# Suffix sums of stick-breaking attention: one fp32 product against two products of a split operand

## The chip, the cores and the metric

The kernel runs on one core of a Trainium2 chip. The metric is device time of that core in microseconds (us), the median of three runs. The engines are named as the profile names them: PE (TensorE, with PEld for its weight loads), DVE (VectorE), ACT (ScalarE), POOL (GpSimd) and SP (SyncE).

## The reference, cut to what matters

The program is a transformer block (SwiGLU, two attentions, SwiGLU, an embedding gate) and four further mixers, at 512 tokens and width 1024. The change touches one of the two attentions of the first block, the stick-breaking one: 8 heads of 64.

```python
z = einsum('bhqd,bhkd->bhqk', q_blk, k) * scale
before = key_pos[None, :] < q_pos[:, None]
log_fail = where(before, log_sigmoid(-z), 0.0)
later = cumsum(log_fail, axis=3, reverse=True) - log_fail
log_a = log_sigmoid(z) + later
a = where(before, exp(where(before, log_a, 0.0)), 0.0)
out = einsum('bhqk,bhkd->bhqd', a, v)
```

With softplus(z) = max(z, 0) + ln(1 + exp(-|z|)), log_fail is -softplus(z), and log_a is z minus the sum of softplus over this key and all later ones. That sum is a product with a triangle of -1 (inside a block of 128 keys) and with a square of -1 (for the later blocks).

## The kernel before

All dense layers run as tiles of 8 k-blocks of weights 128x128. For each k-block `mm3` (L311 on) issues three products of 128x512 (L313 to L315) in the type fp32r, from a weight split in a rounded part `wh` and its rest `wl`. ACT makes `wh` (`split_hi`, L270), DVE makes `wl` (`split_lo`, L280), both three tiles ahead, and DVE takes the result of a tile out of PSUM.

The stage that matters is `mix_in`: 24 tiles that give q, k and v of 16 heads. Its tiles 4 to 14 have the stick-breaking attention woven in. A plan written out by hand, `plan`, says what runs beside which tile: "t" is a transposition of v (L1457, copied out by L1471), "s" a step of the stick-breaking attention, "c" a step of the other attention. `pe_amid` puts the PE part of a step behind a k-block of the tile: of two entries in a tile the first comes behind block 4 and the second behind block 8; of three, behind blocks 2, 5 and 8; a single one behind block 8. The steps in the plan stand so: s0 s1 in tile 4, s2 in 5, s3 s4 in 6, s5 in 7, s6 s7 in 8, s8 in 9, s9 s10 in 10, s11 s12 in 11, s13 in 12, s14 s15 in 13, s16 s17 in 14, s18 in 15; t1, t2, t3, t4 precede the s-steps of tiles 6, 9, 12, 15.

A unit u is a pair of heads and a block of 128 keys (kb = 3, 2, 1, 0), so units of 256, 512, 768 and 1024 columns follow one another, four times over. Its work goes through the engines in order:

- PE, step u: scores z into two PSUM banks (L1327), before that a wait for the weights of unit u-2
- ACT, step u: Abs, Exp, Ln (L1376, L1378, L1380)
- DVE, step u: max(z, 0) plus that (L1365), into the buffer `softplus` of the whole pair
- POOL, step u: a select that zeroes the masked part of the diagonal block (L1395)
- PE, step u+1, behind z of unit u+1: the suffix sums c (L1337), for each of two heads one fp32 product for each key block from kb to 3, added onto z in PSUM: 1, 2, 3 or 4 products for each head, 128 to 512 columns wide
- ACT, step u+1: Exp into `weights` (L1387); POOL selects again (L1401); PE, step u+2: times v (L1350)

The queues are in order. For tile k ACT issues: `split_hi` of tile k+3 (it waits until PE is through with tile k-1, whose buffer it fills), then the steps of tile k. DVE issues: `split_lo` of tile k+3 (it waits for that `split_hi`), then the steps of tile k, then the evacuation of tile k (L1512, L1520, L1523). At steps 6, 10, 14 and 18 DVE also copies a finished pair out of PSUM (L1358), first in the step. POOL runs only the selects and sums of squares here. After tile 23 come the last "c" steps, and then the product with `w_out`.

Of the kernel before, what the change touches and what calls it, by code (L numbers as in the profile page):

```python
# [25 lines left out]
F32 = mybir.dt.float32  # L26
F32R = mybir.dt.float32r
I32 = mybir.dt.int32
ALU = mybir.AluOpType
ACT = mybir.ActivationFunctionType  # L30

P = 128
SEQ = 512
D = 1024
DB = D // P
TB = SEQ // P
# [17 lines left out]
def kernel_program(nc, I, out):  # L54
    top = ExitStack()
    with top:
        def sem(name):
            return top.enter_context(nc.semaphore(name))

        def sb(name, shape, dt=F32, ctx=top):  # L60
            return ctx.enter_context(nc.sbuf_tensor(name, shape, dt))
# [111 lines left out]
        for name, n, src in stages:  # L173
            first[name] = len(tile_stage)
            for k in range(n):
# [4 lines left out]
                if name == "ple" and k % 2:  # L180
                    kb = PLE // P
                elif name.endswith("_down"):
                    kb = min(WB, FB - WB * (k % DOWN))
                else:
                    kb = DB
# [439 lines left out]
        for nm in ("g_ffn1_pre", "g_ffn1_post", "g_mix_pre", "g_mix_post", "g_ffn2_pre", "g_ffn2_post", "g_ple_post",  # L625
                   "g_out_sb", "g_out_ch", "norm_w_2", "final_norm_w_2", "conv_w_conv_2"):
            a = I[nm]
            if len(a.shape) == 1:
                v = a.rearrange("(r c) -> r c", c=P)
            elif len(a.shape) == 2:  # L630
                v = a.rearrange("a (r c) -> (a r) c", c=P)
# [649 lines left out]
        with ExitStack() as c:  # L1281
# [4 lines left out]
            bias = sb("bias", [P, H8, SEQ], ctx=c)  # L1286
            osq = sb("out_squares", [P, 4, SEQ], ctx=c)
            osum = sb("out_square_sums", [P, 2, SEQ], ctx=c)
            tri = sb("tri", [P, 2, P], ctx=c)
            tmp = sb("softplus_parts", [P, 4, SEQ], ctx=c)  # L1290
            ch_room = sb("ch_room", [P, 6, SEQ], ctx=c)
            off = {3: 0, 2: P, 1: 3 * P, 0: 6 * P}
            wide = 10 * P
            SP_ = sb("softplus", [P, 2, wide], ctx=c)
            A = sb("weights", [P, 2, wide], ctx=c)
            b_back = sem("bias_back")
            (n_sq, n_sum, n_mm, n_ms, n_inv, n_rt, n_sp, n_rs, n_f) = (sem(f"mixnorm_{x}") for x in (
                "sq", "sum", "mm", "ms", "inv", "root", "spread", "rstd", "f"))
            (sbc, z_mm, abs_d, exp_d, ln_d, sp_raw, sp_d, c_mm, a_raw, a_d, av_mm, o_d) = (sem(f"sb_{x}") for x in (
                "const", "z", "abs", "exp", "ln", "spraw", "sp", "c", "araw", "a", "av", "o"))  # L1300
            ntri, nones = tri[:, 0, :], tri[:, 1, :]
            ev_mix = n["ev"]
            sb_units = [(pair, kb) for pair in range(4) for kb in (3, 2, 1, 0)]
# [3 lines left out]
            def sb_z(u):  # L1307

                b0 = 4 if u % 2 == 0 else 2
                return banks8[:, b0:b0 + 2, 0:SEQ - sb_units[u][1] * P]  # L1310

            def v_cols(slot, x, s):

# [2 lines left out]
            def sb_pe(pe, s):  # L1316
                if s < SU:
                    pair, kb = sb_units[s]
                    slot, z = pair % 3, sb_z(s)
                    if kb == 3:  # L1320
                        pe.wait_ge(evac, ev_mix + 3 * pair + 2)
                    if s == 1:
                        pe.wait_ge(evac, ev_mix + HEAD + 1)
                    if s >= 2:
                        pe.wait_ge(a_raw, s - 1)
                    for r in range(2):
                        pe.matmul(z[:, r, :], qk[HD * r:HD * r + HD, slot, 1, kb * P:kb * P + P],  # L1327
                                  qk[HD * r:HD * r + HD, slot, 0, kb * P:SEQ], start=True, stop=True).then_inc(z_mm, 1)
                if 1 <= s < SU + 1:
                    u = s - 1  # L1330
                    kb, z = sb_units[u][1], sb_z(u)
                    if u == 0:
                        pe.wait_ge(sbc, 2)
                    pe.wait_ge(sp_d, u + 1)
                    for r in range(2):
                        for k2 in range(kb, TB):
                            m = pe.matmul(z[:, r, (k2 - kb) * P:SEQ - kb * P], ntri if k2 == kb else nones,  # L1337
                                          SP_[:, r, off[k2]:off[k2] + SEQ - k2 * P],
                                          start=False, stop=True, skip_group_check=True)
                    m.then_inc(c_mm, 1)  # L1340
                if 2 <= s < SU + 2:
                    u = s - 2
                    pair, kb = sb_units[u]
                    if kb == 3:
                        pe.wait_ge(taken, taken0 + pair + 1)
                        if pair:
                            pe.wait_ge(o_d, pair)
                    pe.wait_ge(a_d, u + 1)
                    for r in range(2):
                        pe.matmul(ps[OUT][HD * r:HD * r + HD, kb * P:SEQ], v_cols(pair % 3, kb, r),  # L1350
                                  A[:, r, off[kb]:off[kb] + SEQ - kb * P],
                                  start=kb == 3, stop=kb == 0, skip_group_check=True).then_inc(av_mm, 1)

            def sb_dve(dve, s):
                if s >= 6 and s % 4 == 2:
                    pair = s // 4 - 1
                    dve.wait_ge(av_mm, 8 * pair + 8)
                    nc.vector.tensor_copy(F[:, pair, :], ps[OUT][:, :]).then_inc(o_d, 1)  # L1358
                if s < SU:
                    kb = sb_units[s][1]  # L1360
                    w = SEQ - kb * P
                    dve.wait_ge(ln_d, s + 1)
                    if s >= 4:
                        dve.wait_ge(c_mm, s // 4 * 4)
                    nc.vector.scalar_tensor_tensor(out=SP_[:, :, off[kb]:off[kb] + w], in0=sb_z(s),  # L1365
                                                   scalar=0.0, in1=tmp[:, 2 * (s % 2):2 * (s % 2) + 2, 0:w], op0=ALU.max,
                                                   op1=ALU.add).then_inc(sp_raw, 1)

            def sb_act(act, s):
                if s < SU:  # L1370
                    w = SEQ - sb_units[s][1] * P
                    t = tmp[:, 2 * (s % 2):2 * (s % 2) + 2, 0:w]
                    act.wait_ge(z_mm, 2 * s + 2)
                    if s >= 2:
                        act.wait_ge(sp_raw, s - 1)
                    nc.scalar.activation(t, sb_z(s), ACT.Abs).then_inc(abs_d, 1)  # L1376
                    act.wait_ge(abs_d, s + 1)
                    nc.scalar.activation(t, t, ACT.Exp, scale=-1.0).then_inc(exp_d, 1)  # L1378
                    act.wait_ge(exp_d, s + 1)
                    nc.scalar.activation(t, t, ACT.Ln, bias=1.0).then_inc(ln_d, 1)  # L1380
                if 1 <= s < SU + 1:
                    u = s - 1
                    kb = sb_units[u][1]
                    act.wait_ge(c_mm, u + 1)
                    if u >= 4:
                        act.wait_ge(av_mm, u // 4 * 8)
                    nc.scalar.activation(A[:, :, off[kb]:off[kb] + SEQ - kb * P], sb_z(u), ACT.Exp).then_inc(a_raw, 1)  # L1387

            def sb_pool(pool, s):

                if s < SU:
                    kb = sb_units[s][1]
                    v = SP_[:, :, off[kb]:off[kb] + P]
                    pool.wait_ge(sp_raw, s + 1)
                    nc.gpsimd.affine_select(out=v, in_=v, compare_op=ALU.is_gt, fill=0.0, base=0,  # L1395
                                            pattern=[[0, 2], [1, P]], channel_multiplier=-1).then_inc(sp_d, 1)
                if 1 <= s < SU + 1:
                    kb = sb_units[s - 1][1]
                    v = A[:, :, off[kb]:off[kb] + P]
                    pool.wait_ge(a_raw, s)  # L1400
                    nc.gpsimd.affine_select(out=v, in_=v, compare_op=ALU.is_gt, fill=0.0, base=0,  # L1401
                                            pattern=[[0, 2], [1, P]], channel_multiplier=-1).then_inc(a_d, 1)
# [139 lines left out]
                                            ALU.add).then_inc(n_sum, 1)  # L1542

            def pool_tail(pool):
                nc.gpsimd.memset(nones, -1.0).then_inc(sbc, 1)
                pool.wait_ge(sbc, 1)
                nc.gpsimd.affine_select(out=ntri, in_=nones, compare_op=ALU.is_ge, fill=0.0,
                                        base=0, pattern=[[-1, P]], channel_multiplier=1).then_inc(sbc, 1)
                for s in range(SU + 3):
                    sb_pool(pool, s)  # L1550
                    if s >= 6 and s % 4 == 2:
                        pool.wait_ge(o_d, s // 4)
                        out_sums(pool, 0, s // 4 - 1)

                pool.wait_ge(b_back, 16 * (P // COPIES))
                nc.gpsimd.memset(bias[0:HD, :, SEQ - HD:SEQ], NEG).then_inc(sbc, 1)
                pool.wait_ge(n_sum, 3)
                for s in range(CU + 5):
                    ch_pool(pool, s)
                    if s >= 8 and s % 4 == 0:  # L1560
                        pool.wait_ge(o_taken, g_ch + s // 4 - 1)
                        out_sums(pool, 1, s // 4 - 2)
# [1313 lines left out]
```

## Time and profile before

| | us |
|---|---|
| median of 3 runs | 2346.49 |
| lowest, highest | 2342.91, 2348.24 |
| the profiled execution | 2341.71 |
| its span | 2339.9 |
| PE busy | 2211.8 (95%) |
| PE weight loads busy | 1776.7 (76%) |
| DVE busy | 1127.8 (48%) |
| ACT busy | 854.7 (37%) |
| POOL busy | 412.3 (18%) |

A row of the timeline gives the start of an instruction (or of a run of the same ones, with x their number), how long it took, and in brackets the idle time of its engine before it with what ended it. The time of a matmul in the profile is from its start to its modelled end; the pace of products is read from start to start. An fp32 product leaves two records, one in fp32r leaves one. PEclk is the granted clock of PE: 1.00 is 2.4 GHz, 0.50 is 1.2 GHz.

### The profile page before, as it was taken

The numbers are of one execution on the slowest core, as the hardware profiler recorded it, in microseconds if no ns is written. First come the engines' busy times: TensorE is split into PE (matmuls) and PEld (weight loads), VectorE is DVE, ScalarE is ACT, GpSimd is POOL, SyncE is SP. The second block draws the span as 40 slices with busy tenths as digits, with TensorE's granted clock in tenths as the row PEclk, the third lists the DMA queues.
The fourth block names the chain that finished last, engine by engine and source line by source line (L and its number), as shares of the span: only waits on it lengthen the run. The fifth ranks groups of instructions, "written<-read, shape, count | busy, mean of one in ns | idle before, by whom it ended". The sixth has DMA issues, their size and how long they took to land. (4 is left out here: it accounts for less than half of the span.)

```text
span 2339.9 us, 29203 instructions
## 1 busy us (share of the span) xinstructions
PE 2211.8 (95%) x10830; PEld 1776.7 (76%) x10830; DVE 1127.8 (48%) x1805; ACT 854.7 (37%) x1405; POOL 412.3 (18%) x459
## 2 busy tenths in 40 slices
PE   7999999999889999998899999999999997899989
PEld 6888887666677888887788878886777886776657
DVE  5444324423436444324575543346565775655433
ACT  4322223443334322223432241135445753433453
POOL 2111003112423111001210010002100241014441
PEclk8999999999989999999999999999999996999999
DMA  4333333411022333331333256740242220233202
GB/s 135 116 93 96 95 97 84 95 45 55 19 72 72 108 97 94 97 94 50 109 90 99 72 91 97 101 72 1 72 119 74 68 58 10 73 86 73 48 18 70
DMA packets 359321, 182.12 MB, mean 78 GB/s; under 512 B 41925, under 2 KB 356014, under 8 KB 358830
## 3 DMA queue, kind: packets, MB, share of 16 engines
q1 hardware_dynamic: 359214, 180.69, 31.0%
q8 instruction: 68, 1.11, 0.2%
q14 instruction: 39, 0.32, 0.0%
HBM read 176.14 MB, written 4.52 MB: 77 GB/s over the span
## 5 line engine op out<-in xcount | busy, mean ns | idle before, releaser
L313 PE MATMUL ps<-xh,wh 128*128 128x512 f32 x1920 | 766.0, 399 | 10.8 <-DVE wl L280 4.2
L315 PE MATMUL ps<-xh,wl 128*128 128x512 f32 x1920 | 749.3, 390 | 0.0
L314 PE MATMUL ps<-xl,wh 128*128 128x512 f32 x1920 | 748.5, 390 | 0.0
L280 DVE TENSOR_TENSOR wl<-raw,wh 128x1024 fp32r<-128x1024 f32 x334 | 422.6, 1266 | 435.7 <-ACT wh L270 431.0
L270 ACT ACTIVATE wh<-raw 128x1024 fp32r<-128x1024 f32 x334 | 342.1, 1027 | 375.3 <-PE ps L315 332.1
L313 PEld LDWEIGHTS ps<-xh,wh 128*128 128x128 f32 x1920 | 360.9, 188 | 102.9 <-issue 22.2
L315 PEld LDWEIGHTS ps<-xh,wl 128*128 128x128 f32 x1920 | 360.7, 188 | 77.3
L314 PEld LDWEIGHTS ps<-xl,wh 128*128 128x128 f32 x1920 | 361.1, 188 | 73.0 <-issue 2.4
L458 PE MATMUL ps<-xh,wh 128*128 128x512 f32 x304 | 129.9, 427 | 25.4 <-ACT xh L393 15.6
L451 POOL TENSOR_TENSOR acc<-acc,sq 128x512 f32<-128x512 f32 x72 | 102.6, 1424 | 273.1 <-ACT sq L836 178.0
L313 PE MATMUL ps<-a_hi,wh 128*128 128x512 f32 x352 | 136.9, 389 | 0.0
L314 PE MATMUL ps<-a_lo,wh 128*128 128x512 f32 x352 | 136.9, 389 | 0.0
L315 PE MATMUL ps<-a_hi,wl 128*128 128x512 f32 x352 | 136.9, 389 | 0.0
L749 POOL TENSOR_TENSOR F<-F,rstd 128x512 f32<-128x512 f32 x44 | 57.1, 1299 | 400.8 <-ACT F L764 400.8
L459 PE MATMUL ps<-xh,wl 128*128 128x512 f32 x304 | 126.9, 417 | 0.0
L462 PE MATMUL ps<-xl,wh 128*128 128x512 f32 x304 | 91.6, 410 | 4.7 <-DVE xl L426 3.0
L458 PEld LDWEIGHTS ps<-xh,wh 128*128 128x128 f32 x304 | 62.7, 206 | 40.9 <-issue 26.6
L767 ACT ACTIVATE a_hi<-ps 128x512 f32 (+1 forms) x44 | 26.4, 599 | 163.8 <-DVE ps L787 163.8
L764 ACT ACTIVATE F<-ps 128x512 f32<-128x512 f32 x44 | 26.4, 599 | 150.7 <-DVE ps L784 150.7
L448 POOL COPY acc<-sq 128x512 f32<-128x512 f32 x12 | 8.8, 736 | 395.9 <-ACT sq L887 323.4
L315 PEld LDWEIGHTS ps<-a_hi,wl 128*128 128x128 f32 x352 | 66.1, 188 | 13.8
L313 PEld LDWEIGHTS ps<-a_hi,wh 128*128 128x128 f32 x352 | 66.1, 188 | 13.7
(380 smaller groups left out, 2560.7 us busy)
## 6 DMA issues: line engine op xcount, KB each, us to landing
raw<-in_w_ffn_gate SPq DMA_DIRECT2D x44, 512.0 KB, 3.8
raw<-in_w_ffn_up SPq DMA_DIRECT2D x44, 512.0 KB, 3.8
raw<-in_w_ffn_down SPq DMA_DIRECT2D x32, 512.0 KB, 3.8
raw<-in_conv_w_in SPq DMA_DIRECT2D x32, 512.0 KB, 4.0
raw<-in_fox_w_in SPq DMA_DIRECT2D x32, 512.0 KB, 9.9
raw<-in_gdn_w_in SPq DMA_DIRECT2D x32, 512.0 KB, 4.1
raw<-in_w_in SPq DMA_DIRECT2D x24, 512.0 KB, 3.8
raw<-in_swa_w_in SPq DMA_DIRECT2D x32, 256.0 KB, 3.8
```

What stands on the lines that cost most here:

```text
L270: nc.scalar.activation(wh[s][:, 0:kb, :], raw[r][:, 0:kb, :], ACT.Copy).then_inc(hi_done, 1)
L280: nc.vector.tensor_tensor(wl[s][:, 0:kb, :], raw[r][:, 0:kb, :], wh[s][:, 0:kb, :].bitcast(F32), ALU.subtract).then_inc(lo_done, 1)
L313: pe.matmul(o, wh[s][:, kb, :], x_hi, start=start, stop=False)
L314: pe.matmul(o, wh[s][:, kb, :], x_lo, start=False, stop=False)
L315: return pe.matmul(o, wl[s][:, kb, :], x_hi, start=False, stop=stop)
L451: nc.gpsimd.tensor_tensor(acc[:, :], acc[:, :], sq[:, b % 2, :], ALU.add).then_inc(acc_done, 1)
L458: pe.matmul(ps[g][:, :], wh[s][:, b, :], x_hi[:, b, :], start=b == 0, stop=False)
L459: pe.matmul(ps[g][:, :], wl[s][:, b, :], x_hi[:, b, :], start=False, stop=False)
L462: last = pe.matmul(ps[g][:, :], wh[(t + g) % SPLIT][:, b, :], x_lo[:, b, :], start=False, stop=b == DB - 1)
L749: nc.gpsimd.tensor_tensor(SR[:, s, :], S[:, s, :], rstd[:, :], ALU.mult).then_inc(sr_done, 1)
L764: nc.scalar.activation(S[:, s, :], ps[ffn_bank(i, j)][:, :], ACT.Silu).then_inc(silu_done, 1)
L767: nc.scalar.activation(act_hi[:, bass.ds(p, 1), :], ps[ffn_bank(i, j)][:, :].rearrange("p (o q) -> p o q", o=1), ACT.Copy).then_inc(up_hi, 1)
```

## The change

The softplus of a unit is written into `softplus_parts` in place of a buffer of its own, and masked there. From it ACT makes a rounded copy `softplus_hi` in fp32r, at the end of its step u, behind the weights of unit u-1; DVE makes the rest, `softplus_lo`, as the first work (behind a pair's copy) of its step u+1. The triangle and the square of -1 are fp32r, in which they are exact. PE then issues two fp32r products in place of each fp32 one, first the rounded part and then the rest, with the widest key block last instead of first. PE waits for `softplus_lo` where it waited for the select. The `weights` buffer holds two units in turn in place of a pair. Abs and Exp now count on one semaphore, Ln and the rounded copy on another. Nothing changes in the plan.

```diff
@@ -1286,18 +1286,19 @@
             bias = sb("bias", [P, H8, SEQ], ctx=c)
             osq = sb("out_squares", [P, 4, SEQ], ctx=c)
             osum = sb("out_square_sums", [P, 2, SEQ], ctx=c)
-            tri = sb("tri", [P, 2, P], ctx=c)
+            tri = sb("tri", [P, 2, P], F32R, ctx=c)
             tmp = sb("softplus_parts", [P, 4, SEQ], ctx=c)
             ch_room = sb("ch_room", [P, 6, SEQ], ctx=c)
             off = {3: 0, 2: P, 1: 3 * P, 0: 6 * P}
             wide = 10 * P
-            SP_ = sb("softplus", [P, 2, wide], ctx=c)
-            A = sb("weights", [P, 2, wide], ctx=c)
+            sp_hi = sb("softplus_hi", [P, 2, wide], F32R, ctx=c)
+            sp_lo = sb("softplus_lo", [P, 2, wide], F32R, ctx=c)
+            A = sb("weights", [P, 4, SEQ], ctx=c)
             b_back = sem("bias_back")
             (n_sq, n_sum, n_mm, n_ms, n_inv, n_rt, n_sp, n_rs, n_f) = (sem(f"mixnorm_{x}") for x in (
                 "sq", "sum", "mm", "ms", "inv", "root", "spread", "rstd", "f"))
-            (sbc, z_mm, abs_d, exp_d, ln_d, sp_raw, sp_d, c_mm, a_raw, a_d, av_mm, o_d) = (sem(f"sb_{x}") for x in (
-                "const", "z", "abs", "exp", "ln", "spraw", "sp", "c", "araw", "a", "av", "o"))
+            (sbc, z_mm, abs_exp, ln_hi, sp_raw, sp_d, sp_parts, c_mm, a_raw, a_d, av_mm, o_d) = (sem(f"sb_{x}") for x in (
+                "const", "z", "absexp", "lnhi", "spraw", "sp", "parts", "c", "araw", "a", "av", "o"))
             ntri, nones = tri[:, 0, :], tri[:, 1, :]
             ev_mix = n["ev"]
             sb_units = [(pair, kb) for pair in range(4) for kb in (3, 2, 1, 0)]
@@ -1308,6 +1309,12 @@
 
                 b0 = 4 if u % 2 == 0 else 2
                 return banks8[:, b0:b0 + 2, 0:SEQ - sb_units[u][1] * P]
+
+            def sb_t(u, w):
+                return tmp[:, 2 * (u % 2):2 * (u % 2) + 2, 0:w]
+
+            def sb_a(u, w):
+                return A[:, 2 * (u % 2):2 * (u % 2) + 2, 0:w]
 
             def v_cols(slot, x, s):
 
@@ -1331,12 +1338,13 @@
                     kb, z = sb_units[u][1], sb_z(u)
                     if u == 0:
                         pe.wait_ge(sbc, 2)
-                    pe.wait_ge(sp_d, u + 1)
+                    pe.wait_ge(sp_parts, u + 1)
                     for r in range(2):
-                        for k2 in range(kb, TB):
-                            m = pe.matmul(z[:, r, (k2 - kb) * P:SEQ - kb * P], ntri if k2 == kb else nones,
-                                          SP_[:, r, off[k2]:off[k2] + SEQ - k2 * P],
-                                          start=False, stop=True, skip_group_check=True)
+                        for k2 in range(TB - 1, kb - 1, -1):
+                            for part in (sp_hi, sp_lo):
+                                m = pe.matmul(z[:, r, (k2 - kb) * P:SEQ - kb * P], ntri if k2 == kb else nones,
+                                              part[:, r, off[k2]:off[k2] + SEQ - k2 * P],
+                                              start=False, stop=True, skip_group_check=True)
                     m.then_inc(c_mm, 1)
                 if 2 <= s < SU + 2:
                     u = s - 2
@@ -1348,7 +1356,7 @@
                     pe.wait_ge(a_d, u + 1)
                     for r in range(2):
                         pe.matmul(ps[OUT][HD * r:HD * r + HD, kb * P:SEQ], v_cols(pair % 3, kb, r),
-                                  A[:, r, off[kb]:off[kb] + SEQ - kb * P],
+                                  sb_a(u, SEQ - kb * P)[:, r, :],
                                   start=kb == 3, stop=kb == 0, skip_group_check=True).then_inc(av_mm, 1)
 
             def sb_dve(dve, s):
@@ -1356,47 +1364,60 @@
                     pair = s // 4 - 1
                     dve.wait_ge(av_mm, 8 * pair + 8)
                     nc.vector.tensor_copy(F[:, pair, :], ps[OUT][:, :]).then_inc(o_d, 1)
+                if 1 <= s < SU + 1:
+                    u = s - 1
+                    kb = sb_units[u][1]
+                    w = SEQ - kb * P
+                    o = off[kb]
+                    dve.wait_ge(ln_hi, hi_of(u))
+                    nc.vector.tensor_tensor(sp_lo[:, :, o:o + w], sb_t(u, w), sp_hi[:, :, o:o + w].bitcast(F32),
+                                            ALU.subtract).then_inc(sp_parts, 1)
                 if s < SU:
-                    kb = sb_units[s][1]
-                    w = SEQ - kb * P
-                    dve.wait_ge(ln_d, s + 1)
-                    if s >= 4:
-                        dve.wait_ge(c_mm, s // 4 * 4)
-                    nc.vector.scalar_tensor_tensor(out=SP_[:, :, off[kb]:off[kb] + w], in0=sb_z(s),
-                                                   scalar=0.0, in1=tmp[:, 2 * (s % 2):2 * (s % 2) + 2, 0:w], op0=ALU.max,
+                    w = SEQ - sb_units[s][1] * P
+                    dve.wait_ge(ln_hi, ln_of(s))
+                    nc.vector.scalar_tensor_tensor(out=sb_t(s, w), in0=sb_z(s), scalar=0.0, in1=sb_t(s, w), op0=ALU.max,
                                                    op1=ALU.add).then_inc(sp_raw, 1)
+
+            def ln_of(u):
+                return 2 * u + 1
+
+            def hi_of(u):
+                return 2 * u + 2
 
             def sb_act(act, s):
                 if s < SU:
                     w = SEQ - sb_units[s][1] * P
-                    t = tmp[:, 2 * (s % 2):2 * (s % 2) + 2, 0:w]
+                    t = sb_t(s, w)
                     act.wait_ge(z_mm, 2 * s + 2)
                     if s >= 2:
-                        act.wait_ge(sp_raw, s - 1)
-                    nc.scalar.activation(t, sb_z(s), ACT.Abs).then_inc(abs_d, 1)
-                    act.wait_ge(abs_d, s + 1)
-                    nc.scalar.activation(t, t, ACT.Exp, scale=-1.0).then_inc(exp_d, 1)
-                    act.wait_ge(exp_d, s + 1)
-                    nc.scalar.activation(t, t, ACT.Ln, bias=1.0).then_inc(ln_d, 1)
+                        act.wait_ge(sp_parts, s - 1)
+                    nc.scalar.activation(t, sb_z(s), ACT.Abs).then_inc(abs_exp, 1)
+                    act.wait_ge(abs_exp, 2 * s + 1)
+                    nc.scalar.activation(t, t, ACT.Exp, scale=-1.0).then_inc(abs_exp, 1)
+                    act.wait_ge(abs_exp, 2 * s + 2)
+                    nc.scalar.activation(t, t, ACT.Ln, bias=1.0).then_inc(ln_hi, 1)
                 if 1 <= s < SU + 1:
                     u = s - 1
-                    kb = sb_units[u][1]
                     act.wait_ge(c_mm, u + 1)
-                    if u >= 4:
-                        act.wait_ge(av_mm, u // 4 * 8)
-                    nc.scalar.activation(A[:, :, off[kb]:off[kb] + SEQ - kb * P], sb_z(u), ACT.Exp).then_inc(a_raw, 1)
-
-            def sb_pool(pool, s):
-
+                    if u >= 2:
+                        act.wait_ge(av_mm, 2 * u - 2)
+                    nc.scalar.activation(sb_a(u, SEQ - sb_units[u][1] * P), sb_z(u), ACT.Exp).then_inc(a_raw, 1)
                 if s < SU:
                     kb = sb_units[s][1]
-                    v = SP_[:, :, off[kb]:off[kb] + P]
+                    act.wait_ge(sp_d, s + 1)
+                    if s >= 4:
+                        act.wait_ge(c_mm, s // 4 * 4)
+                    nc.scalar.activation(sp_hi[:, :, off[kb]:off[kb] + w], t, ACT.Copy).then_inc(ln_hi, 1)
+
+            def sb_pool(pool, s):
+
+                if s < SU:
+                    v = sb_t(s, P)
                     pool.wait_ge(sp_raw, s + 1)
                     nc.gpsimd.affine_select(out=v, in_=v, compare_op=ALU.is_gt, fill=0.0, base=0,
                                             pattern=[[0, 2], [1, P]], channel_multiplier=-1).then_inc(sp_d, 1)
                 if 1 <= s < SU + 1:
-                    kb = sb_units[s - 1][1]
-                    v = A[:, :, off[kb]:off[kb] + P]
+                    v = sb_a(s - 1, P)
                     pool.wait_ge(a_raw, s)
                     nc.gpsimd.affine_select(out=v, in_=v, compare_op=ALU.is_gt, fill=0.0, base=0,
                                             pattern=[[0, 2], [1, P]], channel_multiplier=-1).then_inc(a_d, 1)
@@ -1542,9 +1563,9 @@
                                             ALU.add).then_inc(n_sum, 1)
 
             def pool_tail(pool):
-                nc.gpsimd.memset(nones, -1.0).then_inc(sbc, 1)
+                nc.gpsimd.memset(nones.bitcast(F32), -1.0).then_inc(sbc, 1)
                 pool.wait_ge(sbc, 1)
-                nc.gpsimd.affine_select(out=ntri, in_=nones, compare_op=ALU.is_ge, fill=0.0,
+                nc.gpsimd.affine_select(out=ntri, in_=nones.bitcast(F32), compare_op=ALU.is_ge, fill=0.0,
                                         base=0, pattern=[[-1, P]], channel_multiplier=1).then_inc(sbc, 1)
                 for s in range(SU + 3):
                     sb_pool(pool, s)
```

## Rows read from the trace of the kernel before

**Rows 1.** Windows: stretch, length, PE, PEld, DVE, ACT, POOL busy, PEclk, DMA, GB/s.

```profile
427.00:548.00 121.00, 120.19 (x542) 80.21 (x542) 35.83 (x42) 54.27 (x74) 19.04 (x37) 1.00 0.26 61
```

**Rows 2.** By tile: one line of kernel each, durations minimum/median/maximum in ns, forms.

```profile
L1337 PE MATMUL ps<-softplus,tri x160: 272/379/697, 430.3 to 545.2; 128*128 128x128 f32 x64, 128*128 128x256 f32 x48, 128*128 128x384 f32 x32, 128*128 128x512 f32 x16
L1365 DVE SCALAR_TENSOR_TENSOR softplus<-ps,softplus_parts x16: 423/824/1225, 428.9 to 538.1; 128x256 f32<-128x256 f32 x4, 128x512 f32<-128x512 f32 x4, 128x768 f32<-128x768 f32 x4, 128x1024 f32<-128x1024 f32 x4
...
L1378 ACT ACTIVATE softplus_parts<-softplus_parts x16: 416/738/1057, 428.0 to 535.9; 128x256 f32<-128x256 f32 x4, 128x512 f32<-128x512 f32 x4, 128x768 f32<-128x768 f32 x4, 128x1024 f32<-128x1024 f32 x4
```

**Rows 3.** Timeline of unit 15, from its scores to its suffix sums.

```profile
533.69 1.13 PE L1327 MATMUL ps<-qk_slots 64*128 64x512 f32 x4
...
534.75 2.87 PE L1337 MATMUL ps<-softplus,tri 128*128 128x384 f32 x12
...
537.54 0.65 PE L1350 MATMUL ps<-weights,v_tokens 128*64 128x256 f32 x4
...
538.13 1.23 DVE L1365 SCALAR_TENSOR_TENSOR softplus<-ps,softplus_parts 128x1024 f32<-128x1024 f32 x1 [5.58 <-ACT softplus_parts L1380]
538.69 1.05 ACT L270 ACTIVATE wh<-raw 128x1024 fp32r<-128x1024 f32 x1
...
539.43 0.41 POOL L1395 TENSOR_SCALAR_AFFINE_SELECT softplus<-softplus 128x256 f32<-128x256 f32 x1 [3.69 <-DVE softplus L1365]
...
539.87 1.41 DVE L280 TENSOR_TENSOR wl<-raw,wh 128x1024 fp32r<-128x1024 f32 x1
...
540.98 4.47 PE L1337 MATMUL ps<-softplus,tri 128*128 128x512 f32 x16
...
545.39 0.87 PE L1350 MATMUL ps<-weights,v_tokens 128*64 128x384 f32 x4
```

**Rows 4.** Timeline: the pace of fp32r products, and of weight loads without columns behind.

```profile
425.31 0.40 PE L315 MATMUL ps<-xh,wl 128*128 128x512 f32 x1
...
425.55 0.39 PE L313 MATMUL ps<-xh,wh 128*128 128x512 f32 x1
...
387.92 0.97 PEld L335 LDWEIGHTS ps<-ones,sq 128*128 128x128 f32 x8
```

**Rows 5.** Timeline: scores and suffix sums of units 2, 3, 7, 10 and 13 on PE.

```profile
436.46 0.92 PE L1327 MATMUL ps<-qk_slots 64*128 64x384 f32 x4
...
444.30 1.13 PE L1327 MATMUL ps<-qk_slots 64*128 64x512 f32 x4
...
445.36 2.87 PE L1337 MATMUL ps<-softplus,tri 128*128 128x384 f32 x12
...
451.43 4.58 PE L1337 MATMUL ps<-softplus,tri 128*128 128x512 f32 x16
...
473.32 1.13 PE L1327 MATMUL ps<-qk_slots 64*128 64x512 f32 x4
...
484.33 4.58 PE L1337 MATMUL ps<-softplus,tri 128*128 128x512 f32 x16
...
497.82 0.92 PE L1327 MATMUL ps<-qk_slots 64*128 64x384 f32 x4
...
504.56 2.87 PE L1337 MATMUL ps<-softplus,tri 128*128 128x384 f32 x12
...
522.78 0.70 PE L1327 MATMUL ps<-qk_slots 64*128 64x256 f32 x4
...
528.85 1.57 PE L1337 MATMUL ps<-softplus,tri 128*128 128x256 f32 x8
```

**Rows 6.** Timeline and windows: two waits of PE of one length, and the clock beside them.

```profile
393.79 0.77 PE L458 MATMUL ps<-xh,wh 128*128 128x512 f32 x1 [2.71 <-ACT xh L393]
...
392.00:395.00 3.00, 1.21 (x3) 1.05 (x4) 2.93 (x5) 1.30 (x3) 1.37 (x2) 0.54 0.87 235
...
1792.57 1.05 PE L2259 MATMUL ps<-ones,gdn_slots 128*128 128x1 f32 x8 [2.71 <-ACT gdn_slots L2089]
...
1792.00:1796.00 4.00, 3.43 (x19) 3.01 (x20) 3.93 (x9) 3.31 (x5) 0.00 (x0) 1.00 0.52 135
```

More of the change, by code:

```diff
@@ L1371, in sb_act @@
                     w = SEQ - sb_units[s][1] * P
-                    t = tmp[:, 2 * (s % 2):2 * (s % 2) + 2, 0:w]
+                    t = sb_t(s, w)
                     act.wait_ge(z_mm, 2 * s + 2)
                     if s >= 2:
-                        act.wait_ge(sp_raw, s - 1)
-                    nc.scalar.activation(t, sb_z(s), ACT.Abs).then_inc(abs_d, 1)
-                    act.wait_ge(abs_d, s + 1)
-                    nc.scalar.activation(t, t, ACT.Exp, scale=-1.0).then_inc(exp_d, 1)
-                    act.wait_ge(exp_d, s + 1)
-                    nc.scalar.activation(t, t, ACT.Ln, bias=1.0).then_inc(ln_d, 1)
+                        act.wait_ge(sp_parts, s - 1)
[4 more added lines that the diff above has]
+                    nc.scalar.activation(t, t, ACT.Ln, bias=1.0).then_inc(ln_hi, 1)
                 if 1 <= s < SU + 1:
                     u = s - 1
-                    kb = sb_units[u][1]
                     act.wait_ge(c_mm, u + 1)
-                    if u >= 4:
-                        act.wait_ge(av_mm, u // 4 * 8)
-                    nc.scalar.activation(A[:, :, off[kb]:off[kb] + SEQ - kb * P], sb_z(u), ACT.Exp).then_inc(a_raw, 1)
+                    if u >= 2:
+                        act.wait_ge(av_mm, 2 * u - 2)
+                    nc.scalar.activation(sb_a(u, SEQ - sb_units[u][1] * P), sb_z(u), ACT.Exp).then_inc(a_raw, 1)
+                if s < SU:
+                    kb = sb_units[s][1]
+                    act.wait_ge(sp_d, s + 1)
+                    if s >= 4:
+                        act.wait_ge(c_mm, s // 4 * 4)
+                    nc.scalar.activation(sp_hi[:, :, off[kb]:off[kb] + w], t, ACT.Copy).then_inc(ln_hi, 1)
             def sb_pool(pool, s):
                 if s < SU:
-                    kb = sb_units[s][1]
-                    v = SP_[:, :, off[kb]:off[kb] + P]
+                    v = sb_t(s, P)
                     pool.wait_ge(sp_raw, s + 1)
```

## The prediction, made before the changed kernel was seen

> **What bounds the kernel now.** First the page: PE is busy 95% of the span, every other engine under half, so time is gained or lost on PE. Then the windows of the stage: from 427 to 548 us, where all sixteen units run, PE is busy 120.19 of 121 us at full clock, ACT 54 and DVE 36 [rows 1]. PE waits for nothing here. Each unit goes through a long chain PE, ACT, DVE, POOL, PE, but the plan puts enough tile products between its two ends. So two numbers decide: how much PE time the suffix sums give back, and whether the cover still holds a chain that grows by two operations and loses part of the cover. The tile and timeline views give both.
>
> **What PE gets back.** L1337 has 160 records, two for each fp32 product: 32 products of 128 columns, 24 of 256, 16 of 384, 8 of 512, 20,480 columns in all [rows 2]. Unit 15 has 2560 columns and takes 4.41 us up to the next product (540.98 to 545.39), unit 14 1536 columns and 2.79 us (534.75 to 537.54) [rows 3]. Four clocks for a column at 2.4 GHz make 4.27 and 2.56; the rest is mostly a change-over that stays. In all that is some 34.3 us.
> After the change there are 160 fp32r products. One of 512 takes 0.227 us to or from its neighbour (425.31 to about 425.55, with rounding), 0.213 of it columns [rows 4]. For 256 and 384 I take the columns and the same 0.013: 0.120 and 0.173. For 128 no fp32r row exists. Each product brings a weight load, and loads with only one column behind them go every 0.11 us, (0.97 - 0.19) / 7 [rows 4]; so a 128-wide product can't be expected under 0.112. Bounds: 0.053 (columns alone) and 0.215 (an fp32 product's four clocks). I take 0.112, the row nearest in what it does. Sum: 64 x 0.112 + 48 x 0.120 + 32 x 0.173 + 16 x 0.227 = 22.1 us. PE work falls by 12.2 us: by nothing in a unit of 256 columns (both heads), 0.36 us at 512, 0.97 at 768, 1.8 at 1024.
> The weight-load row shows 0.11 us. The Trainium skill, TensorE: Matmul & The Clock Gate, section LDWEIGHTS, gives such a load its columns divided by 1.2 GHz, 107 ns, and the trace agrees; the same page's section Back-to-back issue gap gives a product its columns at 2.4 GHz plus 2.5 ns, 56 ns for 128. By that second rule alone the new sums would be an estimated 17.5 us and PE would get back 16.8.
>
> **What the chain becomes.** Unit 15, the plainest [rows 3]: scores start at 533.69; L1365 starts 4.44 us later and takes 1.23; the select ends at 539.84, 6.15 us after the scores. PE came for the sums at 540.98, 7.29 us after the scores, so there was 1.1 us to spare. New behind the select:
> - ACT's rounded copy. Nearest row: `split_hi`, 1.05 us for 1024 columns from and to the same kinds of memory [rows 3]; narrower ones as L1378, 0.42 to 1.06 [rows 2]. I take 1.03, 0.81, 0.60, 0.39 with 0.05 for each hand-over. ACT stands still for it from Ln to the end of the select.
> - DVE's subtraction. Nearest row: `split_lo`, two operands of 1024 columns, 1.41 us beside POOL's work in [rows 3]; I take 1.25, about L1365's 1.225 at that width [rows 2], and 0.97, 0.70, 0.43 for the others.
> Within a tile the widest chain is thus 6.15 + 0.05 + 1.03 + 0.05 + 1.25 + 0.05 = 8.58 us; in the same way 6.97 for 768, 5.36 for 512, 3.76 for 256.
> But the subtraction belongs to DVE's next step. Where that step is in the next tile, the subtraction stands behind `split_lo` of a later tile, which waits for `split_hi`, which now stands behind the rounded copy: 1.05 + 0.05 + 1.27 = 2.37 us more. Behind a pair's copy (L1358) or the copy of v (L1471) it is 0.68 more.
>
> **The sixteen units against their cover.** Cover is the distance from scores to sums on PE, less what the sums of the unit before give back.
> - Unit 15 (1024, next tile): 8.58 + 2.37 = 10.95 against 7.29 - 0.97 = 6.32. PE waits 4.6.
> - Unit 10 (768, next tile): 9.34 against 504.56 - 497.82 - 0.36 = 6.38 [rows 5]. Wait 3.0.
> - Units 13 and 5 (512, next tile, behind a pair's copy): 5.36 + 2.37 + 0.68 = 8.41 against 528.85 - 522.78 = 6.07 [rows 5]. Wait 2.35 each, 4.7 together; the rows of unit 5 stand at the same distance.
> - Unit 7 (1024, next tile, behind v's copy): 11.63 against 484.33 - 473.32 - 0.97 = 10.04 [rows 5]. Wait 1.6.
> - Unit 2 (768, next tile, behind v's copy): 6.97 + 2.37 + 0.68 = 10.02 against 445.36 - 436.46 - 0.36 = 8.54 [rows 5]. Wait 1.5, part of it at the transposition.
> - Unit 3 (1024, same tile): 8.58 against 451.43 - 444.30 - 0.97 = 6.16, and unit 2's wait of 0.9 lies in that cover [rows 5]. Wait 1.5.
> - Unit 0 (256, same tile): 3.76 against three blocks (9 x 0.227) and two scores, about 3.2. Wait 0.5.
> - The other eight have more cover than chain: next tile at 256 or 512 columns with a whole tile or two between, or behind a wait just counted (6, 11, 14).
> Sum of waits 17.4 us, all new, against 12.2 given back: the stage ends 5.2 us later. Nothing queued behind on DVE or ACT makes PE wait further: the splits are three tiles ahead, and a tile's evacuation is wanted two tiles later. POOL's selects move with their inputs. The new copies and subtractions, 11.3 and 13.4 us of work, would be free as engine time; it's their place in the queues that costs. The v product's wait for its buffer is met early, and L1365 loses its wait for the sums of the pair before, which no one is late by. From tile 15 on nothing differs, so the shift goes through to the end.
>
> **The clock.** A wait of 2.71 us before 393.79 had PE at 1.2 GHz behind it (granted 0.54 in 392 to 395), one of 2.71 before 1792.57 did not (1.00 in 1792 to 1796) [rows 6]. Unit 15's 4.6 us is longer than both. I price one fall: 3 us at half clock, as the first of these rows shows, cost PE some 1.5 us of work, and as the row ends before the fall does I take 1.7 (an estimate); nothing is the lower bound, 6 us the upper, for falls at units 10 and 15 of twice that length each. The Trainium skill, same page, section HAM oscillation, says that waits between bursts bring the clock down and every burst starts slow; taken at its word at each wait over 2 us it would be the upper bound.
>
> **Sum.** 5.2 + 1.7 = 6.9 us. The profiled execution took 2341.7 us, so 2348.6 in its terms; it stands 4.8 us under the median of the runs, 2346.5, from which I forecast: 2353.4 us.
>
> **Rivals.**
> - The narrow products don't run at full rate (the change doesn't do all that it says). If 128 columns cost 0.215, the 64 of them take 6.6 us more, of which 2.9 falls into waits: 3.7 later, 2357. For it: no row shows a narrow fp32r product. Against it: nothing in the rows but the name of the type. Chance 0.2.
> - Break-even. The narrow products at 0.06 (3.3 us less, 1.4 of it eaten by longer waits), hand-overs and subtractions a tenth shorter (0.7) and no fall of the clock: 5.2 - 1.9 - 0.7 = 2.6 later, 2349. Chance 0.22.
> - Faster: the saving lands and the waits do not come. One mechanism: the subtraction isn't held up by `split_lo`, because DVE and ACT reach the next tile's splits before PE is through with the tile. That takes away up to 2.37 us at units 15, 10, 13, 5, 7, 2, so 4.6 + 3.0 + 4.7 + 1.6 + 1.5 shrinks to 2.3 + 0.6, with 2.0 for units 3 and 0: 4.9 against 12.2, 7.3 faster, 2339. It decides from waits under 12.2 us in all. Against it: `split_hi` waits for the end of the tile before, and the rows show it at 538.69, behind unit 15's other work [rows 3]. Chance 0.07.
> - The forecast, waits about 17 with little or one fall of the clock: 0.51, its own range 2350 to 2359.
>
> **Range and chances.** The bounds (narrow products at either end, subtraction at 1.41 us for + 0.9, clock 0 to 6) reach from 2348 to over 2362. The range of 2346.5 to 2361.5 leaves out most of the faster case and the worst of the clock. Some 0.2% (4.7 us) is about what a measurement of this kernel can tell from no change. The faster case gives 0.06 over that, break-even 0.22 within it with a sliver of the others, slower 0.72.
>
> **What would show it.** In the profile after: sums of 512 columns 0.227 us apart and of 128 about 0.112 (0.215 makes it the first rival); PE idle before the sums of units 15, 10, 13, 5, in this order, ended by the subtraction; DVE with `split_lo` directly ahead of the subtraction there; ACT idle about 1 us before each rounded copy; PE idle in the stage 15 to 20 us where it was 1. The forecast is wrong if that idle time is under 12 us, if the subtraction runs before `split_lo`, or if the shift at the end of tile 14 isn't the shift at the end of the kernel.

## The result

The changed kernel took 2358.8 us in the median of ten runs (2349.6 to 2362.0) against 2342.8 us for the kernel before in its ten (2339.7 to 2348.9); the ratio is 1.0049, interval 1.0033 to 1.0064, which is 11.5 us slower. The two medians stand further apart, 16.0 us: the times of the change fall into two groups (2349.6 to 2350.8 and 2356.0 to 2362.0), and the median lies in the upper one. Measured again beside the experiments the ratio was 1.0040 (1.0024 to 1.0056). The profiled execution of the change is one of the lower group (2350.3 us); its span is 2348.6 us, 8.7 over that of before.

In the windows (columns as in [rows 1]) the stage that had PE busy 120.19 of 121 us now leaves it idle for 14 us:

```profile
427.00:548.00 121.00, 106.67 (x509) 73.63 (x508) 46.68 (x57) 64.56 (x89) 18.30 (x36) 0.96 0.27 57
```

The waits of PE between 425 and 562 us (total, times, longest) name one releaser, DVE's subtraction:

```profile
PE ps L1345 <- DVE softplus_lo L1373: 15.4, 8, 4.2
PE ps L1478 <- DVE v_features L1533: 1.2, 1, 1.2
```

As the measure of the stage I take the start of unit 0's scores and the start of unit 15's product with v. Before, from the timeline:

```profile
427.01 0.49 PE L1327 MATMUL ps<-qk_slots 64*128 64x128 f32 x4
...
549.12 1.08 PE L1350 MATMUL ps<-weights,v_tokens 128*64 128x512 f32 x4
```

After:

```profile
426.37 0.49 PE L1334 MATMUL ps<-qk_slots 64*128 64x128 f32 x4
...
558.28 1.08 PE L1358 MATMUL ps<-weights,v_tokens 128*64 128x512 f32 x4
```

122.1 us have become 131.9: the stage is 9.8 us longer, and nearly all of it (8.7) is there at the end. Unit 15, which answers to [rows 3], shows the chain in full, from the timeline of the changed kernel:

```profile
539.54 1.13 PE L1334 MATMUL ps<-qk_slots 64*128 64x512 f32 x4
...
543.99 1.22 DVE L1378 SCALAR_TENSOR_TENSOR softplus_parts<-ps,softplus_parts 128x1024 f32<-128x1024 f32 x1 [5.71 <-ACT softplus_parts L1398]
...
545.29 0.41 POOL L1417 TENSOR_SCALAR_AFFINE_SELECT softplus_parts<-softplus_parts 128x256 f32<-128x256 f32 x1 [5.86 <-DVE softplus_parts L1378]
...
545.73 1.06 ACT L1410 ACTIVATE softplus_hi<-softplus_parts 128x1024 fp32r<-128x1024 f32 x1 [1.07 <-POOL softplus_parts L1417]
546.69 1.04 ACT L270 ACTIVATE wh<-raw 128x1024 fp32r<-128x1024 f32 x1
547.83 1.23 DVE L280 TENSOR_TENSOR wl<-raw,wh 128x1024 fp32r<-128x1024 f32 x1 [2.02 <-ACT wh L270]
548.97 1.22 DVE L1373 TENSOR_TENSOR softplus_lo<-softplus_parts,softplus_hi 128x1024 fp32r<-128x1024 f32 x1
...
550.25 0.33 PE L1345 MATMUL ps<-softplus_hi,tri 128*128 128x128 f32 x1 [4.22 <-DVE softplus_lo L1373]
```

The select ends 6.16 us after the scores, as before; then come the rounded copy, `split_hi`, `split_lo` and only then the subtraction, and PE has its sums 10.71 us after the scores.

The other long waits, with the scores of the same unit ahead of each, answer to [rows 5] (units 2, 3, 7, 10, 13; of unit 5, at 470.03, only the first product of its sums is shown):

```profile
436.32 0.92 PE L1334 MATMUL ps<-qk_slots 64*128 64x384 f32 x4
...
446.02 0.33 PE L1345 MATMUL ps<-softplus_hi,tri 128*128 128x128 f32 x1 [0.70 <-DVE softplus_lo L1373]
...
444.18 1.13 PE L1334 MATMUL ps<-qk_slots 64*128 64x512 f32 x4
...
452.73 0.33 PE L1345 MATMUL ps<-softplus_hi,tri 128*128 128x128 f32 x1 [1.55 <-DVE softplus_lo L1373]
...
470.03 0.33 PE L1345 MATMUL ps<-softplus_hi,tri 128*128 128x128 f32 x1 [1.98 <-DVE softplus_lo L1373]
...
474.44 1.13 PE L1334 MATMUL ps<-qk_slots 64*128 64x512 f32 x4
...
485.75 0.33 PE L1345 MATMUL ps<-softplus_hi,tri 128*128 128x128 f32 x1 [1.16 <-DVE softplus_lo L1373]
...
497.44 0.92 PE L1334 MATMUL ps<-qk_slots 64*128 64x384 f32 x4
...
507.17 0.47 PE L1345 MATMUL ps<-softplus_hi,tri 128*128 128x128 f32 x1 [3.32 <-DVE softplus_lo L1373]
...
525.52 0.70 PE L1334 MATMUL ps<-qk_slots 64*128 64x256 f32 x4
...
533.61 0.33 PE L1345 MATMUL ps<-softplus_hi,tri 128*128 128x128 f32 x1 [1.98 <-DVE softplus_lo L1373]
```

The products of unit 14 show the new pace, from 540.60 on one after the other (128, 128, 256, 256, 384, 384 columns for the first head, and from 541.52 on the same for the second):

```profile
540.60 0.33 PE L1345 MATMUL ps<-softplus_hi,tri 128*128 128x128 f32 x1
...
540.88 0.33 PE L1345 MATMUL ps<-softplus_hi,tri 128*128 128x256 f32 x1
...
541.17 0.34 PE L1345 MATMUL ps<-softplus_hi,tri 128*128 128x384 f32 x1
...
541.52 0.22 PE L1345 MATMUL ps<-softplus_hi,tri 128*128 128x128 f32 x1
...
541.69 0.33 PE L1345 MATMUL ps<-softplus_hi,tri 128*128 128x256 f32 x1
...
542.42 0.65 PE L1358 MATMUL ps<-weights,v_tokens 128*64 128x256 f32 x4
```

The unit takes 1.82 us to the next product, where the same unit took 2.79. And three windows show the clock behind three of the waits (PEclk is the third number from the end, behind the five engines):

```profile
505.00:514.00 9.00, 6.83 (x23) 5.19 (x24) 4.57 (x4) 4.06 (x5) 0.98 (x3) 0.62 0.20 58
...
534.00:538.00 4.00, 4.00 (x17) 3.07 (x17) 2.21 (x2) 1.59 (x3) 2.28 (x4) 0.57 0.38 109
...
551.00:555.00 4.00, 4.00 (x16) 2.89 (x14) 0.00 (x0) 0.35 (x1) 0.00 (x0) 0.57 0.28 85
```

They lie behind the waits of units 10, 13 and 15. Behind the waits of units 3 (1.55 us) and 5 (1.98 us), the next longest, no window of the trace shows a fall.

### The profile page after: what moved, and what is told of

It is laid out like the page before. It is cut to its first block and busy times, and to the rows that moved or that the text cites. A ratio compares the mean times of both kernels' runs of the same rounds, so it can differ in the third digit from the quotient of the medians.

```text
span 2348.6 us, 29237 instructions
## 1 busy us (share of the span) xinstructions
PE 2205.9 (94%) x10830; PEld 1776.3 (76%) x10830; DVE 1141.1 (49%) x1821; ACT 865.8 (37%) x1421; POOL 411.5 (18%) x459
## 5 line engine op out<-in xcount | busy, mean ns | idle before, releaser
L458 PE MATMUL ps<-xh,wh 128*128 128x512 f32 x304 | 130.2, 428 | 25.8 <-ACT xh L393 15.8
L451 POOL TENSOR_TENSOR acc<-acc,sq 128x512 f32<-128x512 f32 x72 | 102.5, 1423 | 273.3 <-ACT sq L836 178.0
L458 PEld LDWEIGHTS ps<-xh,wh 128*128 128x128 f32 x304 | 62.9, 207 | 41.1 <-issue 26.7
```

What stands on the lines that cost most here:

```text
L451: nc.gpsimd.tensor_tensor(acc[:, :], acc[:, :], sq[:, b % 2, :], ALU.add).then_inc(acc_done, 1)
L458: pe.matmul(ps[g][:, :], wh[s][:, b, :], x_hi[:, b, :], start=b == 0, stop=False)
```

## The experiments

**1. The products without the longer chain.** DVE writes the rounded softplus itself; the rest is a buffer of zeros.

```diff
-                    pe.wait_ge(sp_parts, u + 1)
+                    pe.wait_ge(sp_d, u + 1)
...
-                    nc.vector.scalar_tensor_tensor(out=sb_t(s, w), in0=sb_z(s), ...
+                    nc.vector.scalar_tensor_tensor(out=sp_hi[:, :, o:o + w], in0=sb_z(s), ...
```

> The 160 fp32r products of the change on the chain of before: DVE writes the rounded softplus itself, POOL masks it, PE waits for the select, and the second product of each pair reads a buffer of zeros, so the rest of the softplus is left out of the sums. Theory (products give back, the longer chain takes more): PE waits stay near those of before (about 1.5 us), the stage ends 10 to 12 us earlier, span about 2329. Rival (the fp32r products themselves or the change of type on PE cost more than was priced): gain under 6 us with no new waits.

Measured: ratio 0.9948 (0.9931 to 0.9966), 12 us faster. In the waits no sum of a unit waits for anything. The stage:

```profile
426.38 0.49 PE L1334 MATMUL ps<-qk_slots 64*128 64x128 f32 x4
...
536.32 1.08 PE L1359 MATMUL ps<-weights,v_tokens 128*64 128x512 f32 x4
```

109.9 us, 12.2 shorter than before. The products alone give back just what was priced. This run keeps the other parts of the change, the `weights` buffer of two units and the shared semaphores, so these cost nothing that shows here.

**2. The chain without the products.** The chain as in the change, and one fp32 product of the rounded part.

```diff
-                            for part in (sp_hi, sp_lo):
-                                m = pe.matmul(z[...], ntri if k2 == kb else nones, part[...],
+                            m = pe.matmul(z[...], (ntri if k2 == kb else nones).bitcast(F32), sp_hi[...].bitcast(F32),
```

> The chain of the change (rounded copy on ACT, subtraction on DVE, PE waits for the rest) with one fp32 product of the rounded part as before, so the rest is left out of the sums. Theory: PE waits about 15 us before the suffix sums of units 15, 10, 13, 5, less at 15 than in the change because unit 14's product covers 1 us more; the stage ends about 14 us later, span 2354 to 2359 with falls of the clock. Rival (the cost of the change lies in its products or clock alone): under 5 us later.

Measured: ratio 1.0102 (1.0079 to 1.0124), 24 us slower. Waits of PE and the stage:

```profile
PE ps L1344 <- DVE softplus_lo L1372: 12.0, 8, 3.2
```

and the timeline:

```profile
426.92 0.49 PE L1334 MATMUL ps<-qk_slots 64*128 64x128 f32 x4
...
564.99 1.08 PE L1357 MATMUL ps<-weights,v_tokens 128*64 128x512 f32 x4
```

138.1 us, 16.0 longer, near the 14 expected. But this isn't all waiting: the waits are 12.0 us where 15 were expected, and behind two of them, at units 5 and 15, the clock falls (PEclk 0.83 in the window 470 to 480, and this one):

```profile
556.00:562.00 6.00, 6.00 (x17) 2.73 (x15) 0.00 (x0) 0.65 (x1) 0.00 (x0) 0.74 0.17 51
```

In the change the same chain makes 15.4 us of waits. The 3.4 us more are cover that the quicker products no longer give: PE waits 1.16 us in the change against 0.19 here at unit 7, 4.22 against 3.23 at unit 15, 1.55 against 0.57 at unit 3 and 3.32 against 2.93 at unit 10, close to the 0.97 and 0.36 us by which the prediction shortened the cover. So runs 1 and 2 (-12.2 and +16.0 us in the stage) can't be added up: their sum of 3.8 us has falls of the clock in it and lacks these 3.4 us, and that it comes near the 4.1 us of run 3 is chance.

The profiled span is 26.7 us longer, so another 10.7 arose outside the stage. It goes with the clock: PEclk is 0.57 in 650 to 690 against 0.74 for about the same work before (634 to 674), 0.86 in 1120 to 1140 against 1.00 (1096 to 1116), and 0.91 in 1810 to 1830 against 1.00 (1785 to 1805). Why the clock fell there in this execution stays open.

**3. PE kept busy in the waits.**

```diff
+                    if u in FILL:
+                        pe.wait_ge(taken, taken0 + FILL[u][0])
+                        for _ in range(FILL[u][1]):
+                            pe.matmul(ps[TURN][:, :], ntri, xh[:, 0, :], start=True, stop=True)
                     pe.wait_ge(sp_parts, u + 1)
```

> The changed kernel with products whose result nobody reads, put into the waits of PE before the suffix sums of units 5, 7, 10, 13 and 15 (9, 5, 12, 9 and 17 of 512 columns, 0.227 us each, a little less than each wait), so that PE does not stand idle there. Theory (waits of 17 us less 12 given back, and falls of the clock on top): no stretch at 1.2 GHz between 420 and 560 us, stage 3 to 5 us shorter than in the change, 5 to 6 us over before, and the spread of the times of the change (2349.6 to 2362.0) narrows to its lower end. Rival (the clock plays no part): time as the changed kernel, ratio to before 1.005.

Measured: ratio 1.0015 (1.0001 to 1.0030), 3.5 us slower than before in place of 9 to 12. The interval is clear of that of the first measurement of the change (1.0033 to 1.0064) and overlaps a little with that of the second (1.0024 to 1.0056). Its windows where the changed kernel had lost the clock, and its stage:

```profile
500.00:514.00 14.00, 13.60 (x67) 9.67 (x66) 6.78 (x6) 8.87 (x12) 3.89 (x6) 1.00 0.13 37
530.00:538.00 8.00, 8.00 (x46) 5.69 (x46) 2.59 (x3) 4.36 (x6) 3.63 (x4) 1.00 0.22 67
546.00:555.00 9.00, 9.00 (x46) 6.05 (x45) 1.92 (x2) 2.08 (x2) 0.41 (x1) 1.00 0.17 49
```

The timeline:

```profile
425.94 0.49 PE L1335 MATMUL ps<-qk_slots 64*128 64x128 f32 x4
...
552.11 1.08 PE L1363 MATMUL ps<-weights,v_tokens 128*64 128x512 f32 x4
```

126.2 us: 4.1 over before, 5.7 under the change. The time up to the subtraction is no shorter, only what fills it differs: 52 products of 0.227 us make 11.8, and 3.5 us of waits are left, 15.3 in all against 15.4. No window between 420 and 560 us shows a lower clock. So the falls of the clock cost the change some 5.7 us in this stage, by one profile of each. One expectation failed: the times still spread from 2344.3 to 2359.1, so the waits of this stage are not what makes most of that spread.

**4. The subtraction ahead of the next `split_lo`.**

```diff
-                if 1 <= s < SU + 1:
+                if 1 <= s < SU + 1 and s - 1 not in LAST.values():
+                    sb_rest(dve, s - 1)
...
+                mix_evac_(dve, i, j, ev0)
+                if 4 * i + j in LAST:
+                    sb_rest(dve, LAST[4 * i + j])
```

> The changed kernel with one move: where a unit's next step lies in the next tile, DVE subtracts right behind the evacuation of the tile, ahead of the next split_lo instead of behind it. Theory (the subtraction's place behind split_hi and split_lo costs 2.4 us at units 15, 10, 13, 5, 7, 2): waits before the suffix sums fall to about 10 us, most left at units 3, 15 and 11, the stage ends 2 us earlier than in before, ratio 0.998 to 1.000. Rival (the two added operations alone make the wait): waits as in the change, within 2 us of its time.

Measured: ratio 0.9979 (0.9967 to 0.9991). The waits of PE:

```profile
PE ps L1345 <- DVE softplus_lo L1380: 7.0, 7, 2.3
```

A window of the same run:

```profile
445.00:460.00 15.00, 12.67 (x55) 8.84 (x54) 3.90 (x6) 8.23 (x11) 1.58 (x4) 0.77 0.12 35
```

And its timeline:

```profile
426.34 0.49 PE L1334 MATMUL ps<-qk_slots 64*128 64x128 f32 x4
...
547.68 1.08 PE L1358 MATMUL ps<-weights,v_tokens 128*64 128x512 f32 x4
```

The waits for the subtraction halve, from 15.4 to 7.0 (about 10 were expected), with not an operation less. The stage, 121.3 us, is 0.8 us shorter than before and not 2, as the clock falls behind the longest wait left, 2.33 us at unit 3. The rival, that the two added operations alone make all of the wait, is out; the 7.0 us left are theirs and the shorter cover's.

**5. And the scores two k-blocks ahead.** PE issues the scores 1.4 us before it comes for the sums of the unit before.

```diff
+                for kind, s in spot(k, b + AHEAD):
+                    if kind == "s":
+                        sb_pe(pe, s, 1)
```

> The run with the early subtraction, and PE besides issues each unit's scores two k-blocks (1.4 us) before it comes for the suffix sums of the unit before, so that the cover grows by 1.4 us. Theory (cover against chain): waits before the suffix sums 3 us in all, at most 1.1 at one unit, no fall of the clock between 420 and 560 us, stage 9 us earlier than in before, ratio 0.995 to 0.997, the full gain of the products nearly kept. Rival (what the early subtraction left is not cover but something else): under 2 us better than the run with the early subtraction alone.

> The changed kernel with only the scores two k-blocks ahead, the subtraction left behind split_lo. Theory (cover against chain): waits fall from 17 to about 8 us (3.2 at unit 15, 1.5 at unit 10, 1.0 at 5 and 13), stage 4 us earlier than in before, less what the clock takes at unit 15: ratio 0.998 to 1.000. Rival (the order on DVE alone matters): time as the changed kernel.

> The kernel of before with the scores two k-blocks ahead, as a control. Theory (before has no waits that more cover could remove but 1.2 us at one transposition): within 1.5 us of before. Rival (the earlier scores help for a reason of their own): 3 us or more faster.

Measured, in this order: 0.9960 (0.9944 to 0.9975) with both moves; 0.9987 (0.9974 to 0.9999) with the scores ahead alone; 0.9997 (0.9982 to 1.0013) for the kernel of before with them. The waits of PE of the first two (the third has none):

```profile
PE ps L1348 <- DVE softplus_lo L1383: 1.7, 3, 0.7
```

```profile
PE ps L1348 <- DVE softplus_lo L1376: 5.9, 5, 2.8
```

So 15.4 us of waits become 7.0 by one move, 5.9 by the other and 1.7 by both, and the control shows that the earlier scores are worth nothing where no chain is late. The stage, taken in the same way, is 112.6 us with both moves, 9.5 shorter than before where 9 were expected, and 120.6 with the scores ahead alone, 1.5 shorter, with falls of the clock behind its two longest waits (1.76 and 2.84 us, at units 10 and 15). With both the version beats both kernels, by 0.40% (9.4 us) against before.

**6. The change again**, on the chip of the last three.

> The changed kernel itself, beside the others on one chip, for its spread and its granted clock. Theory: ratio 1.003 to 1.006, PE waits 15 to 18 us, one to three stretches at 1.2 GHz between 500 and 560 us that the kernel before has not.

Measured: 1.0040 (1.0024 to 1.0056), PE waits of 15.4 us for the subtraction in its profile as well, and three falls of the clock in the stage. But they are not the three of the first profile: here they lie behind units 5 (ahead of the stretch expected; PEclk 0.57 in 470 to 478), 10 and 15 (0.68 in 512 to 516, 0.59 in 549 to 557), and behind unit 13 there is none (1.00 in 533 to 547), although PE waits 1.98 us at unit 5 and at unit 13 in both profiles.

Over all the profiles the stage has ten waits of 1.76 to 2.93 us; six have a fall behind them and four have none. All five waits above 3.2 us have one, and none of the shorter waits, up to 1.57 us, has. In the four profiles of the stage with no wait above 1.6 us (before, runs 1 and 3, both moves) and in the control the clock never falls.

Over its eleven runs the time goes with the granted clock of the run: 0.963 to 0.965 at 2349.8 to 2351.6 us, 0.960 or 0.961 at 2356.1 to 2357.9, 0.957 or 0.958 at 2361.5 and 2362.4. The kernel before goes the same way (0.968 at 2340.1, 0.962 at 2353.2), so part of the spread is not the change's.

## Why the prediction was right, and where not

Forecast were 2353.4 us in a range of 2346.5 to 2361.5, 6.9 us over before; measured are 2358.8, 11.5 us over by the ratio and 8.7 in the profiled executions. The mechanism came as forecast: PE work is given back, and the subtraction, late behind `split_lo`, makes new waits of PE that are longer in sum. The cost of the clock came out larger.

**PE work given back.** Forecast 12.2 us. The four kinds of unit now take 0.59, 1.12, 1.82 and 2.75 us up to the product with v; against 9.45 for the four before that is 6.28, or 12.7 us for the four pairs of heads, and run 1 measured 12.2. By kind of unit, from narrow to wide, 0.05, 0.39, 0.98 and 1.76 us are given back; forecast were nothing, 0.36, 0.97 and 1.8. The price of a narrow product, the widest unknown, came out near the value taken: the two products of 128 columns take 0.28 us for the first head (540.60 to 540.88) and 0.17 for the second (541.52 to 541.69), 0.225 on average, against 2 x 0.112 forecast and 2 x 0.215 for the first rival, which is out. A single one can take less than 0.112 us, which the prediction had ruled out: the product behind 541.52 starts at 541.58. A pair of 256 takes 0.29, where 2 x 0.120 was forecast. The prediction's other estimate, 17.5 us for all the new sums, used a figure that the Trainium skill, TensorE: Matmul & The Clock Gate, section Back-to-back issue gap, gives for an isolated product and says is too small for narrow ones in a stream with weight loads; the rows give about 21.6 us (34.3 - 12.7), near the 22.1 of the sum.

**The chain.** Forecast 10.95 us for unit 15, measured 10.71; for unit 10 9.34, measured 9.73; 13: 8.41 and 8.09; 7: 11.63 and 11.31; 2: 10.02 and 9.70; 3: 8.58 and 8.55. The waits of these six units were forecast, in the same order, at 4.6, 3.0, 2.35, 1.6, 1.5 (with the transposition) and 1.5; the rows give 4.2, 3.3, 2.0, 1.2, 0.7 and 1.55. Unit 5 repeats unit 13 (1.98), and unit 0 waits 0.45 where 0.5 was forecast; these are all eight waits of the trace. The sum of the new waits was 17.4 and is 15.8 (15.4 + 1.2, less the 0.8 us that PE waited at a transposition before). Waits less gain: forecast 5.2, by the rows 15.8 - 12.7 = 3.1, by the filled run 4.1.

**The clock.** This is the term that was mis-sized: 1.7 us, one fall, was taken from bounds of 0 and 6. The profile of the change has falls behind three of its waits, and filling them takes 5.7 us off the stage; the time moves by some 6 to 8 us (1.0015 against 1.0040 and 1.0049). I had counted a fall at unit 15 only, because a wait of 2.71 us had gone either way [rows 6]; unit 13's, of 2.0 us, was enough here. Four waits were forecast over 2 us, and in either profile of the change three of them have a fall behind; which of units 5 and 13 it is, is chance as far as the runs show. So one fall was too few, and the 5.7 us measured lie just under the upper bound of 6. The two errors, 1 to 2 us too much for the waits and 4 too little for the clock, have opposite signs; the first hides part of the second.

**The shift at the end.** As forecast nothing behind tile 14 takes it back: the stage is 9.8 us longer but starts 0.64 earlier, so its end comes 9.2 us later, and the end of the kernel 8.7. That it came out so exactly has luck in it: in run 1 12.8 us earlier at the end of the stage became 10.6 at the end of the kernel, and in run 2 15.9 us later became 26.7, with the clock falling elsewhere.

**The faster rival** named the right place: it said that without `split_lo` ahead of the subtraction the waits would stay under the gain. Run 4 made that so: 7.0 us of waits, under the gain of 12, and the time fell below that of before; in the change itself `split_lo` was ahead in every unit that crosses a tile.

## What to carry to other kernels

Ahead of trading one engine's work for two more operations in a chain that crosses engines, subtract for each unit the chain from the cover that its consumer has, with the queue position of each new operation: here 12 us of PE work were gained, and 16 us of waits came from a chain two operations longer, about half of them (15.4 to 7.0 us) from the place of a subtraction of at most 1.2 us, behind work for three tiles later. Count also that quicker work of the consumer covers less (3.4 us here). The move in the queue and 1.4 us more cover turned the loss into a gain of 9.4 of the 12 us. And on PE a wait can cost more than its length, as the clock may fall behind it: some 5.7 us here beside 16 of waits.

## What had not been expected of the hardware

DVE's two-operand work stretches beside POOL's. The rest of unit 14 (768 columns) took 1.53 us with POOL's L1557 (536.42 to 537.46) and then its L1562 running beside it, that of unit 10 0.94 us without; `split_lo` took 1.86 beside L1562, where the other 13 of its rows between 420 and 562 us, with no work of POOL beside them, took 1.21 to 1.23. From the timeline of the changed kernel:

```profile
395.57 1.35 POOL L451 TENSOR_TENSOR acc<-acc,sq 128x512 f32<-128x512 f32 x1 [0.34 <-ACT sq L397]
395.70 0.73 DVE L407 SCALAR_TENSOR_TENSOR F<-F,half,ps 128x512 f32<-128x512 f32 x1
...
503.90 1.26 POOL L1562 TENSOR_TENSOR out_square_sums<-out_squares 128x512 f32<-128x512 f32 x1
...
504.38 1.86 DVE L280 TENSOR_TENSOR wl<-raw,wh 128x1024 fp32r<-128x1024 f32 x1 [1.80 <-ACT wh L270]
...
506.17 0.94 DVE L1373 TENSOR_TENSOR softplus_lo<-softplus_parts,softplus_hi 128x768 fp32r<-128x768 f32 x1
...
536.75 1.53 DVE L1373 TENSOR_TENSOR softplus_lo<-softplus_parts,softplus_hi 128x768 fp32r<-128x768 f32 x1 [1.50 <-ACT softplus_hi L1410]
537.54 1.88 POOL L1562 TENSOR_TENSOR out_square_sums<-out_square_sums,out_squares 128x512 f32<-128x512 f32 x1
```

Unit 10's chain is the one that came out longer than forecast (9.73 against 9.34), and this `split_lo` is in it. The Trainium skill, GPSIMD Engine Reference, section Specifications, says that POOL shares its SBUF interfaces with DVE and that instructions of DVE with two SBUF inputs contend with it; by that rule, the trace agrees: both stretched instructions read two tensors in SBUF, and L407, which reads one of its two from PSUM, took 0.73 us with POOL's L451 beside it all the time, no more than with POOL idle (0.73 to 0.75 us for its rows of this form). No run here takes POOL's work away to test it.
